# The last chunk of a mixing stage: sums of squares ahead of its values, values ahead of the last dense group

## What is computed

```python
h = rmsnorm(x, norm_mix)
qm, km, vm, om, im, fm, cq, ckv, kr = split(h @ w_in)
hm = rmsnorm(mlstm_chunkwise(qm, km, vm, gates(im, fm))) * sigmoid(om)
lat = concat(rmsnorm(ckv), rope(kr))
qa = rmsnorm(cq) @ mla_w_uq
x += concat(hm, attend(qa, lat)) @ w_out
```

## Time and profile before

| | us |
|---|---|
| median of 3 runs | 3121.93 (3119.97 to 3122.65) |
| the profiled execution | 3125.64 |
| its span, first to last instruction | 3123.9 |
| TensorE busy in the span | 2988.7 (96%) |
| VectorE / ScalarE / GpSimd busy | 1580.6 / 1137.1 / 143.3 |
| mean granted TensorE clock | 0.976 |

### The profile page before, as it was taken

The page is one execution under the profiler, slowest core; times in us unless marked ns, Lnnn a source line. Parts: engine busy times, 40 slices in busy tenths (PEclk is TensorE's granted clock), DMA queues, the critical chain, the costliest instruction groups (busy, mean ns, idle before and its releaser), DMA issues. The chain is left out here.

```text
span 3123.9 us, 46695 instructions
## 1 busy us (share of the span) xinstructions
PE 2988.7 (96%) x19219; PEld 2813.3 (90%) x19219; DVE 1580.6 (51%) x2696; ACT 1137.1 (36%) x2148; POOL 143.3 (5%) x260
## 2 busy tenths in 40 slices
PE   6999989999999999998989999999999999999997
PEld 5998755899999999998989887559999999999997
DVE  6233644564554554456561346445645554454655
ACT  6223423443333223335452333334533233333343
POOL 0000300000000000000000003000000000000000
PEclk9999889999999999998999989999999999999998
DMA  3101243421111111112221021533211111111021
GB/s 128 41 28 45 94 152 105 150 73 55 41 55 41 46 50 54 41 46 82 89 71 41 14 94 56 182 92 137 75 53 41 55 41 55 41 41 54 33 95 70
DMA packets 70742, 215.40 MB, mean 69 GB/s; under 512 B 6522, under 2 KB 43386, under 8 KB 54146
## 3 DMA queue, kind: packets, MB, share of 16 engines
q1 hardware_dynamic: 70530, 212.42, 19.7%
HBM read 193.52 MB, written 18.87 MB: 68 GB/s over the span
## 5 line engine op out<-in xcount | busy, mean ns | idle before, releaser
L223 PE MATMUL psum<-h_chunk,out_weight_parts 128*128 128x352 f32 x2112 | 681.5, 323 | 0.0
L224 PE MATMUL psum<-h_chunk,out_weight_parts 128*128 128x352 f32 x2112 | 677.1, 321 | 0.0
L225 PE MATMUL psum<-h_chunk,out_weight_parts 128*128 128x352 f32 x2112 | 676.4, 320 | 0.0
L2233 DVE SCALAR_TENSOR_TENSOR conv_sum<-u_padded,vectors,conv_sum 128x1024 f32<-128x1024 f32 x176 | 226.3, 1286 | 540.2 <-ACT conv_sum L2085 537.1
L224 PEld LDWEIGHTS psum<-h_chunk,out_weight_parts 128*128 128x128 f32 x2112 | 396.8, 188 | 0.0
L223 PEld LDWEIGHTS psum<-h_chunk,out_weight_parts 128*128 128x128 f32 x2112 | 396.2, 188 | 0.0
L225 PEld LDWEIGHTS psum<-h_chunk,out_weight_parts 128*128 128x128 f32 x2112 | 395.8, 187 | 0.0
L223 PE MATMUL psum<-g_parts,out_weight_parts 128*128 128x352 f32 x960 | 309.3, 322 | 0.0
L224 PE MATMUL psum<-g_parts,out_weight_parts 128*128 128x352 f32 x960 | 309.0, 322 | 0.0
L225 PE MATMUL psum<-g_parts,out_weight_parts 128*128 128x352 f32 x960 | 308.8, 322 | 0.0
L2259 DVE TENSOR_TENSOR x<-x,psum 128x352 f32<-128x352 f32 x528 | 254.9, 519 | 94.3 <-PE psum L225 94.0
(11 more groups left out here) (356 smaller groups left out, 5511.8 us busy)
## 6 DMA issues: line engine op xcount, KB each, us to landing
out_weight_stage<-w_up_dram SPq DMA_DIRECT2D x44, 1024.0 KB, 4.8
out_weight_stage<-w_down_dram SPq DMA_DIRECT2D x22, 1024.0 KB, 4.7
mix_weight_stage<-w_in_dram SPq DMA_DIRECT2D x18, 1024.0 KB, 4.9
pages<-cache_dram SPq DMA_DIRECT2D x64, 288.0 KB, 4.6
out_weight_stage<-w_out_dram SPq DMA_DIRECT2D x16, 1024.0 KB, 6.4
out_weight_stage<-w_gate_dram SPq DMA_DIRECT2D x16, 1024.0 KB, 4.8
pages<-cache_dram SPq DMA_DIRECT2D x64, 160.0 KB, 2.7
x<-x_in_dram SPq DMA_DIRECT2D x6, 1408.0 KB, 11.1
```

What stands on the lines that cost most here:

```text
L223: pe.matmul(out, lhs[0], rhs[0], start=first, stop=False)
L224: pe.matmul(out, lhs[0], rhs[1], start=False, stop=False)
L225: return pe.matmul(out, lhs[1], rhs[0], start=False, stop=last)
L2233: dve.scalar_tensor_tensor(t[:, q, 0:SEQ], row[:, tap:tap + SEQ], w, t[:, q, 0:SEQ], ALU.mult, ALU.add).then_inc(ph["conv_step"], 1)
```

## The change

In the last chunk, TensorE's order becomes dense, `spread`, dense, `scores`, then a new `latent_sums` (the 36 instructions of line 1046, now into one bank), then `values`, and the last dense group behind all. The sums wait only for the evacuation of group 60, whose bank they take, and for the squares' additions. ScalarE takes both roots behind the sums, then squares the last heads' outputs, and only then evacuates the last group. VectorE takes the reciprocals ahead of `outputs(7)`. The roots and reciprocals move into free columns of `m_columns` (`cwc`), outside the tile that they had. TensorE's nine transposes stay last, behind the evacuation of the last group.

```diff
--- before.py
+++ after.py
@@ -608,6 +608,7 @@
         ring = WeightRing(None, ph, "mix_projection", stages=1, stage=mem.mix_stage, parts=mem.mix_parts, ready=ready)
         first_third = 1 if l else 0
         LATE = KX * (2 - first_third)
+        SUM_GROUP = len(GROUPS) - 3
         ps = core.psum
 
         def bank(g):
@@ -806,11 +807,12 @@
                 decayed_scores(c)
                 if 4 <= c < 7:
                     latent_squares(c)
+                if c == NCK - 1:
+                    dve.wait_ge(ph["rt_step"], 2)
+                    dve.reciprocal(mem.rt_inverse, mem.rt).then_inc(ph["rs_made"], 1)
                 outputs(c)
                 if c in (1, 3):
                     ring.lo(dve, 7 + c // 2, JW)
-            dve.wait_ge(ph["rt_step"], 2)
-            dve.reciprocal(mem.rt[:, 1], mem.rt[:, 0]).then_inc(ph["rs_made"], 1)
 
         @block.scalar
         def _(act):
@@ -924,13 +926,15 @@
                 if 4 <= c < 7:
                     latent_squares(c)
                 evacuate(MIXED + 3 * c + 1)
-                evacuate(MIXED + 3 * c + 2)
-                if c == NCK - 1:
-                    for i, d in enumerate((Q_RANK, KV_RANK)):
-                        act.wait_ge(ph["lsum_done"], i + 1)
-                        act.activation(mem.rt[:, 0, i, :], ps[:, i, 0:TT], ACT.Sqrt, bias=core.eps,
-                                       scale=1.0 / d).then_inc(ph["rt_step"], 1)
-                squares(c)
+                if c < NCK - 1:
+                    evacuate(MIXED + 3 * c + 2)
+                    squares(c)
+            act.wait_ge(ph["lsum_done"], 1)
+            for i, d in enumerate((Q_RANK, KV_RANK)):
+                act.activation(mem.rt[:, :, i], ps[:, bank(SUM_GROUP), TT * i:TT * (i + 1)], ACT.Sqrt,
+                               bias=core.eps, scale=1.0 / d).then_inc(ph["rt_step"], 1)
+            squares(NCK - 1)
+            evacuate(len(GROUPS) - 1)
 
         @block.tensor
         def _(pe):
@@ -1008,6 +1012,16 @@
                     mm = pe.matmul(ps[part(h), B_UPD, (h // 2) * DV1:(h // 2 + 1) * DV1],
                                    kw[:, c % 2, h * 64:(h + 1) * 64], vTM[:, c, h, :], start=True, stop=True)
                 mm.then_inc(ph["upd_done"], 1)
+
+            def latent_sums():
+                pe.wait_ge(ph["bank_free"], SUM_GROUP + 1)
+                for i, squares in enumerate((core.norm, mem.sqk)):
+                    pe.wait_ge(ph["lsq_added"], 2 + i)
+                    for c in range(TT):
+                        n = TT * i + c
+                        mm = pe.matmul(ps[:, bank(SUM_GROUP), n:n + 1], squares[:, token_tile(c)],
+                                       core.ones[:, 0:1], start=(n == 0), stop=True, skip_group_check=True)
+                mm.then_inc(ph["lsum_done"], 1)
 
             if not ready:
                 pe.wait_ge(ph["lo_made"], 1)
@@ -1037,19 +1051,17 @@
                 spread(c)
                 dense(MIXED + 3 * c + 1)
                 scores(c)
-                dense(MIXED + 3 * c + 2)
-                values(c)
+                if c < NCK - 1:
+                    dense(MIXED + 3 * c + 2)
+                    values(c)
+            latent_sums()
+            values(NCK - 1)
+            dense(len(GROUPS) - 1)
             pe.wait_ge(ph["bank_free"], len(GROUPS))
-            pe.wait_ge(ph["lsq_added"], 3)
-            for i, squares in enumerate((core.norm, mem.sqk)):
-                for c in range(TT):
-                    mm = pe.matmul(ps[:, i, c:c + 1], squares[:, token_tile(c)], core.ones[:, 0:1],
-                                   start=(c == 0), stop=True, skip_group_check=True)
-                mm.then_inc(ph["lsum_done"], 1)
             pe.wait_ge(ph["rs_made"], 1)
             for c in range(TT):
                 tr = pe.transpose(ps[:, c // 4, c % 4 * P:(c % 4 + 1) * P],
-                                  mem.rt[:, 1, 0, c:c + 1].to_broadcast([P, P]), core.ident)
+                                  mem.rt_inverse[:, c, 0:1].to_broadcast([P, P]), core.ident)
             tr.then_inc(ph["rows_done"], 1)
 
 
@@ -1069,7 +1081,7 @@
     krot = at(M_KROT, "k_rotated", [P, NT])
     cs = at(M_CS, "rope_cos_sin", [P, 2, NT])
     hrt = at(M_KROT + NT, "h_rms", [P, 2, 4 * TT])
-    rt, c0 = mem.rt, mem.c0
+    c0 = mem.c0
     og = at(M_KN, "og_all", [P, 4, NT])
     take = core.slab.bump(M_UQ + 4 * 768, M_CS)
     kw = take("ks_weighted", [NS, 256])
@@ -1207,7 +1219,7 @@
                 for c in range(TT):
                     out = ps[:, RB[1] + c // 4, c % 4 * P:(c % 4 + 1) * P] if c < TT - 1 else \
                         ps[:, TAIL[1][0], TAIL[1][1]:TAIL[1][1] + P]
-                    tr = pe.transpose(out, rt[:, 1, 1, c:c + 1].to_broadcast([P, P]), core.ident)
+                    tr = pe.transpose(out, mem.rt_inverse[:, c, 1:2].to_broadcast([P, P]), core.ident)
                 tr.then_inc(ph["rb_done"], 1)
 
             def numerators():
@@ -2790,7 +2802,6 @@
         self.sqt = at(M_QR + NT, "one_square", [P, NT])
         self.c0 = at(M_KN + 4 * NT, "state_sample", [P, DEC_BATCH, 2, DV1])
         self.uq = at(M_KN + 4 * NT + DEC_BATCH * 2 * DV1, "q_weight_stage", [P, 2, 768])
-        self.rt = at(M_KROT + NT + 72, "mla_rt", [P, 2, 2, TT])
         self.H = Halves(at(M_CATM, "h_high", [P, KX, NT], F32R), at(X_AT, "h_low", [P, KX, NT], F32R))
         self.mix_parts = at(M_KN, "mix_weight_parts", [P, 2, 2, JW], F32R)
         self.mix_stage = at(M_QR, "mix_weight_stage", [P, 1, JW])
@@ -2807,6 +2818,7 @@
         self.vTM = at(M_V, "m_v", [P, TT, M_HEADS, DV1])
         self.rows = at(M_ROWS, "m_rows", [64, NT])
         self.cwc = at(M_CWC, "m_columns", [P, TT, 96])
+        self.rt, self.rt_inverse = self.cwc[:, :, 4:6], self.cwc[:, :, 6:8]
         self.hS = at(M_HS, "m_h_sample", [P, M_HEADS, M_DV])
         self.ssq = at(M_SSQ, "m_ssq", [P, 4 * TT])
```

## The result

The changed kernel's median is 3132.8 us (3130.90 to 3136.90 in 6 runs). The kernel before, on the same chip, gave 3122.74 (3119.97 to 3124.81 in 6 runs). The ratio is 1.0032, with a 95% interval of 1.0021 to 1.0042: slower by 10.1 us, where the forecast was 8.5. The profiled execution of the kernel after took 3130.92 us, with a span of 3129.1.

What follows compares the result with a forecast made beforehand. TensorE, busy 96%, was taken to bound the kernel. Per layer 17.6 + 4.4 = 22.0 us against 18.61 and 16.86, together +8.5: 3121.93 + 8.5 = 3130.4 us, range 3123 to 3134.5.

Steps and rivals of the forecast that it cites:

- the forecast's own: End of the mixing stage: sums bring the clock down, values and dense group pay; +8.5 us, chance 0.72.
- Rival A: Clock holds through values and last dense group because TensorE never idles: 2.4 us less, 3119.5 us; chance 0.10.
- Rival B: Clock falls but is back when the last dense group starts, which takes 3.98: +4.5 us per layer, 3126.4; chance 0.10.
- Rival C: The stage's end is shorter, 3.1 us, because the store transfer does not set it: +5.9, 3127.8 us; chance 0.04.
- Rival D: Next stage's first dense products stay at half clock longer: +2 to +4 on top of 8.5, 3132.4 to 3134.4; chance 0.04.
- sums: Sums directly behind the scores: 4.34 us at full clock, 5.2 with a fall inside them; 4.8 taken per layer.
- values: Values behind the sums: 7.0 us all at half clock (3.83 x 1.83); 6.8 taken, since a late fall leaves some full.
- dense group: Last dense group behind the values: 5.6 to 6.0 us while the clock returns, 6.0 taken; 7.0 if it does not.
- to the next stage: From dense group's end: evacuation, gate store, then state's store queued behind it (3.2), plus barrier (1.2): 4.4 us per layer.
- the step that failed: Placing the clock's fall 3.3 us into the sums, as in layer 1 before; the sums' other 1.04 us would cost 1.9.
- The alternative named there: The clock falls only in the values, so the sums stay at 4.34 us.
- What was costed at nothing: ScalarE's squares before the last evacuation (margin 1.2 us), decayed scores covered by 4.3 us of sums, reciprocals, roots, next stage's pause.

Runs made afterwards that it cites:

- Experiment 7: The changed kernel with each latent's nine one-column sums replaced by one nine-column matmul over its first token tile, leaving work out: 3117.71 us, ratio 0.9985.
- experiment 6: The changed kernel with the state's store put ahead of the gate's last store in SP's queue: 3128.0 us, ratio 1.0023 to the kernel before.
- experiment 3: Against the changed kernel, the last dense group ahead of the values, so only the sums moved from the kernel before: 3132.0 us, ratio 1.0029.
- experiment 8: Against the changed kernel, only the first latent's 18 sums stay between scores and values, the other 18 behind the last dense group: 3126.6 us, ratio 1.0016.
- experiments 1 and 2: The changed kernel with sums woven one by one into the dense group ahead of the scores: 3145.1 us, ratio 1.0076; profiled again in another execution: 3142.95 us.
- experiment 2: Second profiled execution of the changed kernel with sums woven one by one into the dense group ahead of the scores: 3142.95 us.

## Why the prediction came out

**The time.** 3130.4 was forecast and 3132.8 measured, inside the range. The case that happened is the forecast's own: the clock falls behind the sums, stays low through the values, and dense products bring it back. Experiment 7 shows that the sums are the cause and not the order alone. Rival A fell (clock 0.50 over most of the values). Rival B fell (the group took 6.0 and 6.1, not 4.0). Rival C fell: the transposes ended at 320.69 and 2.71 us of pause followed, which the store's place changed (experiment 6). Rival D fell: the next stage's first dense product came 6.99 and 6.63 us into it, as before, and the clock rose 4.0 and 4.2 us behind them (means 0.90 and 0.69), where before it was 3.7 and 4.7.

Rival A rested on a reading of the Trainium skill, "TensorE: Matmul & The Clock Gate", section "Why this matters for your kernels". It advises against PE-idle gaps between matmul bursts. The trace does not agree that this is enough, since the clock fell in the kernel after with PE busy 2.00 of 2.00.

**The terms, per layer.** Forecast and found (layer 0, layer 1), us:

| step | forecast | found |
|---|---|---|
| sums | 4.8 | 4.04, 4.04 |
| values | 6.8 | 6.31, 6.24 |
| dense group | 6.0 | 6.0, 6.1 |
| to the next stage | 4.4 | 4.6, 4.9 |
| all | 22.0 | 21.0, 21.3 |

- *Sums, too high by 0.8.* For 0.3 of it the price was wrong: 4.34 adds two durations of 2.17, which overlap, while from start to start 18 sums take 2.03 (302.38 to 304.41). For the rest, the step that failed took the fall 3.3 us into the sums, from layer 1 before. It came 4.7 and 4.8 us behind their start, when they were done. The alternative named there, a fall in the values, is the one that happened. The time isn't fixed: the same block, with only the store moved, fell 3.1 us in in layer 1 of experiment 6, and the sums took 4.9 there.
- *Values, too high by 0.5.* The factor of 1.83 from the earlier trace rows was not theirs. Two pairs of values at half clock start 0.73 apart (309.49 to 310.22) and at full 0.42 (experiment 7), a factor of 1.74. And 0.7 us of them ran at full clock.
- *Dense group, right.* It ran 4.6 and 4.8 us at half clock. The values at half clock before it had not brought the clock back. How long dense products then take isn't fixed either: 3.4 us in experiment 3, where they already ran when it fell. In the earlier trace rows the mean of 0.77 puts the rise before at 332.92, not 333.08, so 3.7 us instead of 3.8; that changes no term.
- *Stage end, too low by 0.2 to 0.5.* The mechanism, the state's store behind that of the gate, was right.
- *What was costed at nothing.* ScalarE's squares left 3.56 us in front of the evacuation, so the margin was wider than the 1.2 claimed. The decayed scores stayed covered. One cost was missed: VectorE waited 0.56 us for the update at half clock, without effect on TensorE.

**The sum.** The chain grew by 6.85 us, where 8.5 was forecast, and the median by 10.1 (6.6 to 13.1 by the interval). So the forecast was 1.6 us too high for the chain and 1.6 too low for the median: 3 us of the slowdown are not in the profiled chain. Part of that may be chance, since the chain's 6.85 lies inside the interval. Part may lie in which executions were profiled: that of the kernel before took 2.9 us more than its median (3125.64 against 3122.74), that of the kernel after 1.9 less (3130.92 against 3132.8), and the two differ by only 5.3. Code that is the same in both took 303.63 us before and 302.38 after up to the changed place in layer 0, and 305.77 in experiment 8. And the clock does not fall alike in all executions of one kernel (experiments 1 and 2); the slowest run of the kernel after, 3136.90, has a mean granted clock of 0.974, the profiled one 0.976. What share each has was not measured.

So the mechanism was right, while it is partly luck that the median came within 2.4 us of the forecast: the errors of the terms add up to a chain that is 1.6 too long, and what the chain doesn't hold made up for it.

## What to carry over

Before a block of small matmuls is moved, look at what will run behind it. At the end of the stage the low clock fell on the sums themselves, nine transposes and the opening of the next stage; in front of values and a dense group it cost 4.4 us per layer, and an engine shown fully busy is no sign that the clock holds. Price such a move by the rows at half clock of the very form that will stand behind it, and compare medians, because the place of the fall differs between executions. Before you ask what a median holds beyond the profile, see how far each profiled execution lies from its own median.

## What the runs showed of the hardware

- Weaving hides nothing: a dense product with two one-column instructions takes 0.38 us (299.79 to 300.17), the product alone 0.16 and the two 0.22.
- A mixture of 352-column products and sums, one to one (experiments 1 and 2), brought the clock down in three of the four layers profiled, and it then stayed down for 13.7 to 27.3 us.
- Values (129 columns) brought the clock neither down in the kernel before nor back in the kernel after: 5.6 us of them at half clock, and it stayed at 0.50. Dense products brought it back 4.6 and 4.8 us into them. Values at full clock were not always safe: in layer 1 of experiment 2, not long after a low stretch, it fell 2.1 us into them.
- The nine transposes take 1.20 us at full clock (319.49) and 2.18 at half.
